# An encoder layer with mixture of experts: raw first rows with the norm in the copies, later small loads, an earlier overflow branch and a last norm in four pieces

## The chip, the cores and the metric

The kernel runs on one core of one Trainium2 chip. The metric is the device time of one execution in microseconds. It was 1304.65 us, the median of three runs (1300.25 to 1307.12).

## What is computed

One layer over 256 tokens of width 1024, in float32. A root-mean-square norm feeds a wide projection. Its parts go through a state-space branch (convolution over time, SiLU, two scan directions, gate) and an attention branch (8 query heads, 2 key/value heads, rotary angles). The two are gated and projected, and added to x. A second norm feeds a router that picks 4 of 32 experts for every token; each expert is two matrices with a clipped gated activation. The weighted sum is added to x, and a last norm gives the result.

```python
def rmsnorm(x, g):
    y = x * lax.rsqrt(jnp.mean(x * x, axis=-1, keepdims=True) + NORM_EPS)
    return y * g

def reference(x, ...):
    x = x + token_mixer(rmsnorm(x, g_mix), w_in, conv_w, ..., w_out)
    x = x + moe_ffn(rmsnorm(x, g_ffn), w_router, b_router, w_mlp1, b_mlp1, w_mlp2, b_mlp2)
    return rmsnorm(x, g_final)
```

## The kernel before

The five engines run programs of their own, written out by hand in one function, `encoder_layer`, and joined by semaphores. SP issues the large loads, ACT issues the small ones ahead of its own work, PE multiplies and transposes, ACT and DVE move results out of PSUM, and POOL computes the inverse roots (`rsqrt_mean`, L951 to L954: scale and add, then power).

Weights stream through `ring`, 16 slots of 1 MB. In the mixer ten slots are used, and the 36 units of the mixer (256 columns of a matrix with 1024 rows each) go through them in order (L333 to L337). SP starts with three waits: for x, for the five parameter rows and for b1. It issues ten units without a wait, then one for each unit that PE has finished. PE's `unit` (L420 to L437) multiplies a unit of weights with the transposed activations `hT` (L433) or the other way round (L436): 16 products of 256 columns, each of two instructions, into bank 0 or 1. A unit may start when ACT has taken the unit before the last one out of its bank (`unit_taken`).

The start is a chain. ACT issues x, the constants `cst` (736 KB), five parameter rows into `prm`, d_skip, b1, wdt, seven broadcast vectors and the router weights, L755 to L768. It squares both halves of x (L773), POOL makes the factors, DVE scales both halves into `hN` (L984), PE transposes 16 tiles of `hN` into banks 2 to 5 (`to_T`, L416), and DVE copies them out with g_mix into `hT` (`scaled_T`, L995), four copies of 128x512. Only then does unit 0 start. In front of `to_T` PE transposes the parameters (L400, L401) and b1 (L405, 16 transposes of 32 rows into bank 7). ACT copies those to `prmT` and `b1T` (L775, L777).

After the mixer comes the routing, and then the 32 experts, 12 units of 1 MB each, with SP keeping the ring full (L328). Eight of the units are the first matrix (`up_unit`) and four the second (`down_unit`); L629 holds their products, L663 the transposes of the result in between. The tokens of an expert are gathered by small products (L611), at most 64 of them per pass, and its output is added into banks 4 to 7 by `combine` (L624). More than 64 tokens for one expert would need a second pass; a flag `over_i` tells whether there is one, and each engine branches on it behind the experts (L924, L1304). With these inputs the pass isn't taken.

The end is a chain too. PE's last four `combine` products signal `c_psum`; DVE waits for all four, adds the banks to `xres` (L1288), reads the flag and branches (L1304), and signals ACT with a one-column copy (L1322). ACT squares both halves (L939), POOL makes the factors, DVE multiplies each half with factor and g_final (L1326), and SP stores each half when it is ready (L388, L390).

Of the kernel before, what the change touches and what calls it, by code (L numbers as in the profile page):

```python
# [7 lines left out]
ALU = mybir.AluOpType  # L8
# [3 lines left out]
P = 128  # L12
# [17 lines left out]
NE = 32  # L30
# [27 lines left out]
C_ID, C_LE, C_GE, C_ONE, C_NEGF, C_ZERO, C_NEGB = (P * i for i in range(7))  # L58
# [33 lines left out]
def encoder_layer(nc, x, g_mix, w_in, conv_w, conv_b, dt_bias_f, dt_bias_b, a_log_f, a_log_b, d_skip,  # L92
                  g_ssm, q_norm_g, k_norm_g, w_br_ssm, w_br_attn, w_out, g_ffn, w_router, b_router,
                  w_mlp1, b_mlp1, w_mlp2, b_mlp2, g_final, consts, out):
    with ExitStack() as ctx:
# [84 lines left out]
        gfin = arena[:, 5888:6912]  # L180
        msk = arena[:, 6912:6976].rearrange("p (t e) -> p t e", t=TT)
# [22 lines left out]
        c_in = sem("c_in"); x_in = sem("x_in"); row_in = sem("row_in"); b1_in = sem("b1_in")  # L204
# [5 lines left out]
        xsq_ready = sem("xsq_ready"); xr_ready = sem("xr_ready"); h_ready = sem("h_ready")  # L210
# [32 lines left out]
        over_step = sem("over_step"); over_left = sem("over_left"); over_even = sem("over_even")  # L243
        fsq_ready = sem("fsq_ready"); fr_ready = sem("fr_ready"); fin_ready = sem("fin_ready"); sum_done = sem("sum_done")
# [53 lines left out]

        def chain(eng, semaphore, base=0):
# [18 lines left out]
        def _(sp):  # L318
# [12 lines left out]
            sp.wait_ge(x_in, 16)  # L331
            sp.wait_ge(row_in, 16 * 5)
            sp.wait_ge(b1_in, 16)  # L333
# [53 lines left out]
            sp.wait_ge(fin_ready, 1)  # L387
            sp.dma_start(out[0, 0:P, :], hN[:, 0, :]).then_inc(out_done, 16)  # L388
            sp.wait_ge(fin_ready, 2)
            sp.dma_start(out[0, P:SEQ, :], hN[:, 1, :]).then_inc(out_done, 16)  # L390
            sp.wait_ge(out_done, 32)
# [3 lines left out]
        def _(pe):  # L395

            pe.wait_ge(c_in, 16)
            pe.wait_ge(row_in, 16 * 5)
            pe.wait_ge(dsk_ready, 1)
            nc.tensor.transpose(bank[6][:, 0:N_ROWS], prm[0:N_ROWS, :], ident[0:N_ROWS, 0:N_ROWS])  # L400
            nc.tensor.transpose(bank[6][:, N_ROWS:N_ROWS + 8], dske[:, :], ident[0:8, 0:8]).then_inc(prm_ready, 1)  # L401
            pe.wait_ge(b1_in, 16)
            for m in range(16):
                o = (m // KD) * KD + spot(m % KD)
                last = nc.tensor.transpose(bank[7][:, o * NE:(o + 1) * NE], b1raw[:, m * P:(m + 1) * P],  # L405
                                           ident[0:NE, 0:NE])
            last.then_inc(prm_ready, 1)

            def to_T(ready, psum_sem):

# [30 lines left out]
            for n in range(U_XBC, U_Z):  # L441
                unit(n, rhs=hT)
# [912 lines left out]
```

## Time and profile before

| | us |
|---|---|
| median of three runs | 1304.65 |
| lowest, highest | 1300.25, 1307.12 |
| span of the profiled execution | 1303.6 |
| PE busy | 1182.3 (91%) |
| PE weight loads busy | 578.6 (44%) |
| DVE busy | 364.2 (28%) |
| ACT busy | 193.1 (15%) |
| POOL busy | 19.9 (2%) |
| read from HBM | 443.61 MB, 341 GB/s over the span |
| share of the last chain | PE 40%, DMA 37%, SP's issues 16%, issue 2%, DVE 2% |

The profile is of one execution, and its times run from 0 at its first instruction to 1303.6 us. A busy share is a mean over stages with different limits. PE is busy for 91% of the span, yet in the last chain it has 40%, since in the long stage of the experts a product that waits for its weights and the stream of the weights take turns. L numbers are lines of the kernel. A wait in brackets behind a row is the idle time of the engine before it, and what ended it.

### The profile page before, as it was taken

How to read it: one execution, taken by the hardware profiler on the slowest of the kernel's cores; microseconds unless marked ns; L12 is line 12 of the kernel's file. 1: busy time of each engine (PE TensorE's matmuls, PEld its weight loads, DVE VectorE, ACT ScalarE, POOL GpSimd, SP SyncE). 2: the span in 40 equal slices, each digit the busy share in tenths (PEclk: the TensorE clock that was granted, in tenths of full speed). 3: DMA queues.
4: the chain of work that ended last, by engine and by line, in shares of the span. 5: the costliest groups of instructions: out<-in, count | busy, mean ns of one | idle time of the engine just before them, and what ended most of it. 6: DMA issues, size and time to landing. Idle time of an engine off the chain costs nothing.

```text
span 1303.6 us, 18034 instructions
## 1 busy us (share of the span) xinstructions
PE 1182.3 (91%) x6734; PEld 578.6 (44%) x6734; DVE 364.2 (28%) x1018; ACT 193.1 (15%) x362; POOL 19.9 (2%) x32
## 2 busy tenths in 40 slices
PE   5999999998799999989998988888899989998885
PEld 5888888887433333333333333333333333333331
DVE  2515788121412221222121111111122212111112
ACT  1212344001111110111011100100111011001001
POOL 0001111000000000000000000000000000000000
PEclk9999999999699999999999999999999999999998
DMA  9944322654099999999999999999999999999994
GB/s 283 281 142 117 128 97 97 230 217 171 29 417 417 417 417 417 417 417 418 417 418 418 418 418 418 418 418 417 417 417 418 418 418 418 418 418 417 418 417 178
DMA packets 113351, 445.18 MB, mean 342 GB/s; under 512 B 9731, under 2 KB 46947, under 8 KB 80515
## 3 DMA queue, kind: packets, MB, share of 16 engines
q1 hardware_dynamic: 109408, 441.48, 85.0%
q10 hardware_dynamic: 3907, 3.21, 0.9%
q8 instruction: 24, 0.39, 0.1%
q14 instruction: 12, 0.10, 0.0%
HBM read 443.61 MB, written 1.05 MB: 341 GB/s over the span
## 4 chain that ended last, share of the span: by engine, by line
PE 40%; DMA 37%; SPq 16%; issue 2%; DVE 2%; ACT 1%; ACTq 1%; DVEq 0%; POOL 0%; POOLq 0%
DMA ring<-in_w_mlp_dram 37%; SPq L328 16%; PE bank L433 14%; PE bank L629 14%; PE bank L436 5%; PE bank L624 1%; PE bank L611 1%; PE bank L562 1%; PE bank L552 1%; PE bank L698 1%; PE bank L524 1%; PE bank L416 1%; PE bank L663 0%; PE bank L591 0%; PE bank L515 0%
## 5 line engine op out<-in xcount | busy, mean ns | idle before, releaser
L629 PE MATMUL bank<-ring,arena 128*64 128x512 f32 x3072 | 702.7, 600 | 63.7 <-DMA ring<-in_w_mlp_dram 63.6
L629 PEld LDWEIGHTS bank<-ring,arena 128*64 128x64 f32 x3072 | 203.0, 137 | 515.3 <-issue 324.2
L1245 DVE TENSOR_TENSOR arena<-bank,b1T 128x256 f32<-128x256 f32 x128 | 53.8, 420 | 624.3 <-PE bank L663 621.9
L433 PE MATMUL bank<-hT,ring 128*128 128x256 f32 x576 | 128.3, 384 | 0.8 <-DVE hT L995 0.8
L433 PEld LDWEIGHTS bank<-hT,ring 128*128 128x128 f32 x576 | 110.9, 193 | 16.6 <-DVE hT L995 1.2
L436 PE MATMUL bank<-ring,hT 128*128 128x256 f32 x320 | 72.1, 386 | 2.2 <-DVE hT L1156 2.2
L906 ACT ACTIVATE arena<-bank 128x512 f32<-128x512 f32 x32 | 19.1, 597 | 362.4 <-PE bank L629 362.3
L436 PEld LDWEIGHTS bank<-ring,hT 128*128 128x128 f32 x320 | 61.5, 194 | 11.1 <-DVE hT L1156 2.6
L624 PE MATMUL bank<-arena 64*128 64x512 f32 x264 | 65.6, 615 | 0.8 <-ACT arena L916 0.8
L611 PEld LDWEIGHTS bank<-slotP,hb 128*128 128x128 bf16 x1536 | 47.7, 99 | 27.1 <-issue 23.5
L611 PE MATMUL bank<-slotP,hb 128*128 128x64 bf16 x1536 | 51.5, 195 | 3.1 <-DVE arena L1229 3.1
L663 PE MATMUL bank<-cst,arena 128*128 128x128 f32 x256 | 40.6, 286 | 14.4 <-ACT arena L906 9.6
L663 PEld LDWEIGHTS bank<-cst,arena 128*128 128x128 f32 x256 | 26.8, 140 | 47.1 <-ACT arena L906 36.1
L1227 DVE TENSOR_SCALAR slotP<-cst,rankm 128x64 bf16<-128x64 f32 x64 | 15.8, 247 | 96.9 <-ACT arena L914 96.9
L911 ACT ACTIVATE arena<-arena 128x256 f32<-128x256 f32 x64 | 26.7, 417 | 80.5 <-DVE arena L1248 80.4
L916 ACT ACTIVATE arena<-bank 128x512 f32<-128x512 f32 x32 | 19.1, 598 | 105.5 <-PE bank L629 105.5
L914 ACT ACTIVATE arena<-bank 128x256 f32<-128x256 f32 x32 | 12.3, 384 | 140.8 <-PE bank L618 140.8
L624 PEld LDWEIGHTS bank<-arena 64*128 64x128 f32 x264 | 22.7, 186 | 22.6 <-issue 20.9
L906 ACT ACT_TABLE_LOAD x8 | 10.3, 1283 | 134.4 <-PE bank L629 134.4
L433 PE MATMUL bank<-arena,ring 128*128 128x256 f32 x128 | 28.3, 380 | 0.5 <-ACT arena L867 0.5
L1251 DVE SCALAR_TENSOR_TENSOR arena<-arena 128x256 f32<-128x256 f32 x64 | 27.2, 426 | 2.4 <-DVE arena L1249 0.2
L433 PE MATMUL bank<-over,ring 128*128 128x256 f32 x128 | 27.8, 379 | 0.0
(204 smaller groups left out, 634.3 us busy)
## 6 DMA issues: line engine op xcount, KB each, us to landing
ring<-in_w_mlp_dram SPq DMA_DIRECT2D x384, 1024.0 KB, 22.1
ring<-in_w_in_dram SPq DMA_DIRECT2D x24, 1024.0 KB, 10.3
ring<-in_w_br_attn_dram SPq DMA_DIRECT2D x4, 1024.0 KB, 4.9
ring<-in_w_br_ssm_dram SPq DMA_DIRECT2D x4, 1024.0 KB, 5.0
ring<-in_w_out_dram SPq DMA_DIRECT2D x4, 1024.0 KB, 5.0
xres<-in_x_dram ACTq DMA_DIRECT2D x1, 1024.0 KB, 4.9
out_dram<-hN SPq DMA_DIRECT2D x2, 512.0 KB, 2.7
cst<-shape_constants_dram ACTq DMA_DIRECT2D x1, 736.0 KB, 6.4
```

The costliest lines, as they stand in the source:

```text
L328: sp.dma_start(dst, src).then_inc(slot_full[s], 16)
L433: last = nc.tensor.matmul(o, w[:, k, a * P:(a + 1) * P], rhs[:, k, :], start=(k == 0), stop=(k == KD - 1))
L436: last = nc.tensor.matmul(o, tokens[:, k, a * P:(a + 1) * P], w[:, k, :], start=(k == 0), stop=(k == KD - 1))
L611: last = nc.tensor.matmul(bank[b][:, k * CAP:(k + 1) * CAP], hb[part][:, t, k * P:(k + 1) * P], slotP[:, par, t, :], start=(t == 0 and par ...
L624: return nc.tensor.matmul(bank[b0 + q][:, :], slotWT[rows, (q // 2) * P:(q // 2 + 1) * P], ysb[rows, :], start=start, stop=stop, skip_grou ...
L629: return nc.tensor.matmul(bank[b][side * CAP:(side + 1) * CAP, :], tokens, w, start=start, stop=stop, skip_group_check=True)
L663: last = nc.tensor.transpose(bank[b][:, j * P:(j + 1) * P], hs[:, b * 512 + j * P:b * 512 + (j + 1) * P], ident)
L906: nc.scalar.activation(hs[:, 0:512], bank[0][:, :], ACT.Copy).then_inc(hs_ready, 1)
L911: nc.scalar.activation(sg[:, h * 256:(h + 1) * 256], ga[:, h * 256:(h + 1) * 256], ACT.Sigmoid, scale=ALPHA).then_inc(sg_ready, 1)
L916: nc.scalar.activation(ysb, bank[2][:, :], ACT.Copy).then_inc(ys_ready, 1)
L1245: step(V.tensor_tensor(o.rearrange("p (m s) -> p m s", m=4), bank[b][:, half].rearrange("p (m s) -> p m s", m=4), bias[:, m0:m0 + 4].unsqu ...
L1251: step(V.scalar_tensor_tensor(u_, u_, 1.0, g_, ALU.add, ALU.mult))
```

## The change

The start: SP drops its three waits and issues x itself, in two halves with a semaphore each, ahead of the weights. ACT first issues only the first 256 columns of the constants, now identity and ones, then the parameter rows and d_skip; b1, wdt, the vectors, the router weights and the rest of the constants are issued behind the squares and the parameter copy. A square of one column stands in front of the squares. PE transposes the raw x as its halves come. The factors of the norm reach the transposed side as a row: DVE writes them on two diagonals (`sqb`), PE multiplies ones with them, DVE copies the product into `rB`, and eight copies of 128x256 multiply the transposed x with g_mix and `rB`. Unit 0 (`first_unit`) goes through k outside and its two column halves inside, waiting for one copy at a time. The transposes of b1 move behind unit 3, and so does ACT's copy of them.

The end: the branch on the overflow flag stands in front of the sums on DVE, and the pass behind it uses banks 0 to 3 instead of 4 to 7. Sums, squares and stores go in four pieces of 128x512. The product with g_final is made on DVE before the factors are known, and the factors are then multiplied in by DVE for two pieces and ACT for two.

```diff
-C_ID, C_LE, C_GE, C_ONE, C_NEGF, C_ZERO, C_NEGB = (P * i for i in range(7))
+C_ID, C_ONE, C_LE, C_GE, C_NEGF, C_ZERO, C_NEGB = (P * i for i in range(7))
+C_FIRST = 2 * P
...
-            sp.wait_ge(x_in, 16)
-            sp.wait_ge(row_in, 16 * 5)
-            sp.wait_ge(b1_in, 16)
+            for t in range(TT):
+                sp.dma_start(xres[:, t, :], x[0, t * P:(t + 1) * P, :]).then_inc(x_in[t], 16)
...
+            for q in range(4):
+                sp.wait_ge(fin_ready[q], 1)
+                sp.dma_start(out[0, (q // 2) * P:(q // 2 + 1) * P, (q % 2) * 512:(q % 2 + 1) * 512], fin(hN, q)).then_inc(out_done, 16)
+            sp.wait_ge(out_done, 16 * 4)
...
+            pe.wait_ge(first_in, 16)
+            for t in range(TT):
+                pe.wait_ge(x_in[t], 16)
+                for k in range(KD):
+                    nc.tensor.transpose(bank[2 + k // 2][:, (k % 2) * 256 + t * P:(k % 2) * 256 + (t + 1) * P],
+                                        xres[:, t, k * P:(k + 1) * P], ident)
+            pe.wait_ge(row_in, 16 * 5)
+            pe.wait_ge(dsk_ready, 1)
+            nc.tensor.transpose(bank[6][:, 0:N_ROWS], prm[0:N_ROWS, :], ident[0:N_ROWS, 0:N_ROWS])
+            nc.tensor.transpose(bank[6][:, N_ROWS:N_ROWS + 8], dske[:, :], ident[0:8, 0:8]).then_inc(prm_ready, 1)
+            pe.wait_ge(xdiag_ready, 1)
+            nc.tensor.matmul(bank[7][:, 0:SEQ], ones, sqb, start=True, stop=True).then_inc(xrB_psum, 1)
+
+            def first_unit():
+
+                mix_full(pe, 0)
+                w = k_view(mix_slot(0))
+                for k in range(KD):
+                    pe.wait_ge(hT_ready, k + 1)
+                    for a in range(2):
+                        last = nc.tensor.matmul(bank[0][:, a * 256:(a + 1) * 256], w[:, k, a * P:(a + 1) * P], hT[:, k, :],
+                                                start=(k == 0 and a == 0), stop=(k == KD - 1), skip_group_check=True)
+                last.then_inc(unit_done, 1)
...
-            for n in range(U_XBC, U_Z):
+            first_unit()
+            for n in range(U_XBC + 1, U_Z):
                 unit(n, rhs=hT)
+                if n == U_XBC + 3:
+                    b1_transposes()
...
-            act.dma_start(xres[:, :, :], x[0].rearrange("(t p) d -> p t d", p=P)).then_inc(x_in, 16)
-            act.dma_start(cst[:, :], consts).then_inc(c_in, 16)
+            act.dma_start(cst[:, 0:C_FIRST], consts[:, 0:C_FIRST]).then_inc(first_in, 16)
...
+            act.wait_ge(pool_step, 2)
+            nc.scalar.activation(stat[:, 22:23], stat[:, 40:41], ACT.Square)
+            for t in range(TT):
+                act.wait_ge(x_in[t], 16)
+                nc.scalar.activation(hN[:, t, :], xres[:, t, :], ACT.Square, accum_out=stat[:, t:t + 1]).then_inc(xsq_ready, 1)
+            act.wait_ge(prm_ready, 1)
+            nc.scalar.activation(prmT[:, :], bank[6][:, 0:N_ROWS + 8], ACT.Copy).then_inc(prm_taken, 1)
             act.dma_start(b1raw, b_mlp1[0]).then_inc(b1_in, 16)
...
+            act.dma_start(cst[:, C_FIRST:N_CONST], consts[:, C_FIRST:N_CONST]).then_inc(c_in, 16)
...
+            for q in range(4):
+                act.wait_ge(c_added, q + 1)
+                nc.scalar.activation(fin(squares, q), fin(xres, q), ACT.Square, accum_out=stat[:, 28 + q:29 + q]).then_inc(fsq_ready, 1)
+            for t in range(TT):
+                act.wait_ge(fr_ready, t + 1)
+                act.wait_ge(xg_ready, 2 * t + 2)
+                nc.scalar.activation(fin(hN, 2 * t + 1), fin(hN, 2 * t + 1), ACT.Copy, scale=stat[:, 36 + t:37 + t]).then_inc(fin_ready[2 * t + 1], 1)
...
+            for t in range(TT):
+                pool.wait_ge(fsq_ready, 2 * t + 2)
+                link(nc.gpsimd.tensor_tensor(stat[:, 36 + t:37 + t], stat[:, 28 + 2 * t:29 + 2 * t], stat[:, 29 + 2 * t:30 + 2 * t], ALU.add))
+                rsqrt_mean(36 + t, 1, D).then_inc(fr_ready, 1)
...
             dve.wait_ge(xr_ready, 1)
-            for t in range(TT):
-                V.tensor_scalar(hN[:, t, :], xres[:, t, :], stat[:, t:t + 1], None, ALU.mult).then_inc(h_ready, 1)
-            dve.wait_ge(c_in, 16)
+            dve.wait_ge(first_in, 16)
+            for t in range(TT):
+                last = V.tensor_scalar(sqb[:, t * P:(t + 1) * P], ident, stat[:, t:t + 1], None, ALU.mult)
+            last.then_inc(xdiag_ready, 1)
+            dve.wait_ge(xrB_psum, 1)
+            link(V.tensor_copy(rB, bank[7][:, 0:SEQ]))
+            dve.wait_ge(prm_taken, 1)
+            for k in range(KD):
+                V.scalar_tensor_tensor(hT[:, k, :], bank[2 + k // 2][:, (k % 2) * 256:(k % 2 + 1) * 256], prmT[:, R_GMIX + k:R_GMIX + k + 1],
+                                       rB, ALU.mult, ALU.mult).then_inc(hT_ready, 1)
...
             dve.wait_ge(gfin_in, 16)
-            for t in range(TT):
-                V.scalar_tensor_tensor(hN[:, t, :], xres[:, t, :], stat[:, 30 + t:31 + t], gfin, ALU.mult, ALU.mult).then_inc(fin_ready, 1)
+            for q in range(4):
+                dve.wait_ge(c_psum, q + 1)
+                V.tensor_tensor(fin(xres, q), fin(xres, q), bank[SUMS + q][:, :], ALU.add).then_inc(c_added, 1)
+            dve.wait_ge(c_added, 4)
+            for t in range(TT):
+                for q in (2 * t + 1, 2 * t):
+                    V.tensor_tensor(fin(hN, q), fin(xres, q), gfin[:, (q % 2) * 512:(q % 2 + 1) * 512], ALU.mult).then_inc(xg_ready, 1)
+            dve.wait_ge(xg_ready, 4)
+            for t in range(TT):
+                dve.wait_ge(fr_ready, t + 1)
+                V.tensor_scalar(fin(hN, 2 * t), fin(hN, 2 * t), stat[:, 36 + t:37 + t], None, ALU.mult).then_inc(fin_ready[2 * t], 1)
```

## Rows read from the trace of the kernel before

**Rows 1.** The page's 40 equal slices: GB/s that the DMAs moved.
```profile
GB/s 283 281 142 117 128 97 97 230 217 171 29 417 417 417 417 417 417 417 418 417 418 418 418 418 418 418 418 417 417 417 418 418 418 418 418 418 417 418 417 178
```

**Rows 2.** Windows: length; busy PE, PEld, DVE, ACT, POOL; PEclk, DMA, GB/s.
```profile
352.00:355.00 3.00, 3.00 (x7) 0.77 (x8) 1.58 (x7) 0.00 (x0) 0.00 (x0) 0.50 0.00 0
358.00:362.00 4.00, 4.00 (x20) 1.26 (x18) 0.00 (x0) 0.00 (x0) 0.00 (x0) 1.00 1.01 397
```

**Rows 3.** Timeline, first 45 us: start, length, engine, line, operation, idle before.
```profile
0.73 0.44 ACTq L755 DMA_DIRECT2D xres<-in_x_dram  x1
...
3.76 0.32 ACTq L761 DMA_DIRECT2D dskr<-in_d_skip_dram  x1
...
8.95 1.28 ACT L773 ACT_TABLE_LOAD   x1 [8.95 <-issue]
9.29 0.21 DVE L979 COPY dske<-dskr 8x128 f32<-8x128 f32 x1 [9.29 <-DMA dskr<-in_d_skip_dram]
9.57 36.26 SPq L337 DMA_DIRECT2D ring<-in_w_in_dram  x13
...
10.10 1.89 PE L405 MATMUL bank<-cst,over 32*128 32x32 f32 x16
10.24 1.06 ACT L773 ACTIVATE hN<-xres 128x1024 f32<-128x1024 f32 x1
...
13.62 1.42 DVE L984 TENSOR_SCALAR hN<-xres,stat 128x1024 f32<-128x1024 f32 x2 [4.12 <-POOL stat L954]
...
15.10 3.67 PE L416 MATMUL bank<-cst,hN 128*128 128x128 f32 x16 [3.10 <-DVE hN L984]
...
19.55 25.79 PE L433 MATMUL bank<-hT,ring 128*128 128x256 f32 x108 [0.78 <-DVE hT L995]
```

**Rows 4.** DMA issues of the kernel: tile, engine, count, size, median us to landing.
```profile
ring<-in_w_out_dram SPq DMA_DIRECT2D x4, 1024.0 KB, 5.0
xres<-in_x_dram ACTq DMA_DIRECT2D x1, 1024.0 KB, 4.9
out_dram<-hN SPq DMA_DIRECT2D x2, 512.0 KB, 2.7
```

**Rows 5.** Landing of unit 0's weights, line L337, issued at 9.57.
```profile
DMA to landing us min/median/max: 9.0/9.0/9.0
```

**Rows 6.** Timeline of the tail, from 1288 us to the end.
```profile
1288.37 1.99 PE L624 MATMUL bank<-arena 64*128 64x512 f32 x8 [0.78 <-ACT arena L916]
...
1290.43 2.48 DVE L1288 TENSOR_TENSOR xres<-xres,bank 128x512 f32<-128x512 f32 x4 [8.35 <-PE bank L624]
1294.48 0.15 DVE L1322 COPY cnt<-cnt 128x1 f32<-128x1 f32 x1 [1.57 <-issue]
1294.66 1.06 ACT L939 ACTIVATE hN<-xres 128x1024 f32<-128x1024 f32 x1 [6.35 <-DVE cnt L1322]
...
1296.94 0.19 POOL L953 TENSOR_SCALAR stat<-stat 128x2 f32<-128x2 f32 x1 [973.61 <-ACT hN L939]
...
1297.94 2.48 DVE L1326 SCALAR_TENSOR_TENSOR hN<-xres,stat,arena 128x1024 f32<-128x1024 f32 x2 [3.31 <-POOL stat L954]
...
1300.45 0.36 SPq L390 DMA_DIRECT2D out_dram<-hN  x1
```

**Rows 7.** Groups by shape, DVE: line, operation, shapes, count, busy, mean ns.
```profile
L1127 DVE SCALAR_TENSOR_TENSOR over<-over,prmT,bank 128x256 f32<-128x256 f32 x8 | 3.8, 472 | 1.8 <-PE bank L552 1.8
...
L1145 DVE TENSOR_SCALAR arena<-cst,stat 128x128 f32<-128x128 f32 x2 | 0.5, 281 | 0.0
```

**Rows 8.** L433 alone in windows: length; busy PE, PEld; PEclk, DMA, GB/s.
```profile
19.55:24.05 4.50, 4.50 (x11) 3.60 (x12) 1.00 1.10 349
24.05:28.95 4.90, 4.90 (x24) 4.33 (x23) 1.00 1.10 348
```

**Rows 9.** Timeline, 214 to 217 us, one DVE line twice.
```profile
214.38 1.10 DVE L1099 TENSOR_TENSOR arena<-arena 128x512 f32<-128x512 f32 x1
...
216.69 0.69 DVE L1099 TENSOR_TENSOR arena<-arena 128x512 f32<-128x512 f32 x1
```

More of the change, by code:

```diff
@@ L180, in encoder_layer @@
         gfin = arena[:, 5888:6912]
+        squares = hs.rearrange("p (t d) -> p t d", t=TT)
         msk = arena[:, 6912:6976].rearrange("p (t e) -> p t e", t=TT)
@@ L203, in encoder_layer @@
         unit_done = sem("unit_done")
-        c_in = sem("c_in"); x_in = sem("x_in"); row_in = sem("row_in"); b1_in = sem("b1_in")
+        c_in = sem("c_in"); first_in = sem("first_in"); x_in = [sem(f"x_in{t}") for t in range(TT)]; row_in = sem("row_in"); b1_in = sem("b1_in")
         vec_in = sem("vec_in"); dsk_in = sem("dsk_in"); wdt_in = sem("wdt_in"); late_in = sem("late_in")
@@ L242, in encoder_layer @@
         over_y = sem("over_y"); over_ys = sem("over_ys"); over_c = sem("over_c"); over_added = sem("over_added")
-        over_step = sem("over_step"); over_left = sem("over_left"); over_even = sem("over_even")
-        fsq_ready = sem("fsq_ready"); fr_ready = sem("fr_ready"); fin_ready = sem("fin_ready"); sum_done = sem("sum_done")
+        over_wT = sem("over_wT"); over_step = sem("over_step"); over_left = sem("over_left"); over_even = sem("over_even")
+        fsq_ready = sem("fsq_ready"); fr_ready = sem("fr_ready"); fin_ready = [sem(f"fin_ready{q}") for q in range(4)]
         def mix_slot(n):
@@ L297, in k_view, with fin @@
             return ring[:, s, :].rearrange("p (k n) -> p k n", k=KD)
+        def fin(tile, q):
+            return tile[:, q // 2, (q % 2) * 512:(q % 2 + 1) * 512]
         def chain(eng, semaphore, base=0):
@@ L418, in to_T, with b1_transposes @@
                     last.then_inc(psum_sem, 1)
-            to_T(h_ready, hT_psum)
+            pe.wait_ge(first_in, 16)
[19 more added lines that the diff above has]
+                last.then_inc(unit_done, 1)
+            def b1_transposes():
+                pe.wait_ge(b1_in, 16)
+                for m in range(16):
+                    o = (m // KD) * KD + spot(m % KD)
+                    last = nc.tensor.transpose(bank[7][:, o * NE:(o + 1) * NE], b1raw[:, m * P:(m + 1) * P],
+                                               ident[0:NE, 0:NE])
+                last.then_inc(prm_ready, 1)
             def unit(n, rhs=None, tokens=None):
@@ L728, in _ @@
                                 o = spot(m % KD) * CAP
-                                last = nc.tensor.matmul(bank[4 + m // 8][:, o:o + CAP],
+                                last = nc.tensor.matmul(bank[m // 8][:, o:o + CAP],
                                                         ring[:, k, m * P:(m + 1) * P], x32[:, k, :],
@@ L738, in _ @@
                                 o = (k % 2) * D + side * 512
-                                last = half_product(0, side, act32[:, spot(k), :], ring[:, k // 2, o:o + 512],
+                                last = half_product(2, side, act32[:, spot(k), :], ring[:, k // 2, o:o + 512],
                                                     k == 0, k == KD - 1)
@@ L793, in _ @@
                     silu(u - 1)
+                if u == 3:
+                    b1_copy()
             silu(5)
@@ L929, in _ @@
                         act.wait_ge(over_x, n)
-                        nc.scalar.activation(slotWT, bank[7][:, 0:256], ACT.Copy)
+                        nc.scalar.activation(slotWT, bank[2][:, 0:256], ACT.Copy).then_inc(over_wT, 1)
                         act.wait_ge(over_ga, n)
```

60 lines of the change are left out of this document (16 added, 44 removed).

## The prediction

> **What bounds the kernel now.** I read four views in this order. The slices of the page come first [rows 1]. From the twelfth slice to the last but one the DMA engines move 417 to 418 GB/s without a gap: this is the stream of 32 experts' weights, 12 MB each. It starts when the PE gives back the first ring slot of expert 0. In the window from 352 to 355 us nothing moves, and from 358 us it is 397 GB/s [rows 2]. From there to the last weights the stream never pauses, so the end of the kernel is the time of that first release, plus a constant, plus what follows the last weights. Two stretches are therefore worth money one for one: the chain up to the experts, and the tail.
>
> The chain up to the experts is a dependency chain, not a transfer. Its start is in the timeline of the first 20 us [rows 3]. ACT spends the time up to 8.95 us issuing small loads, loads its table (1.28 us) and starts the first square at 10.24 us, though x had landed 4.9 us after its issue at 0.73, at about 5.6 us [rows 4]. Then come POOL, two DVE scalings at 13.62, sixteen PE transposes at 15.10, four DVE copies, and the first projection unit starts at 19.55 us. It waited for hT, not for weights: SP issued the first weights at 9.57 us and they landed 9.0 us later, at 18.57 [rows 3, 5]. From then on PE is the busiest engine of the mixer, and DVE and ACT work in its wake, so a start that is S us earlier moves the whole mixer by S.
>
> The tail is in the timeline after 1288 us [rows 6]: PE combines from 1288.37 to 1290.36, four DVE sums from 1290.43 (waiting for all four products), the overflow branch on DVE (1.57 us idle before the copy at 1294.48), two ACT squares, POOL, two DVE scalings from 1297.94, and stores, the last issued at 1300.45 and landing 2.7 us later [rows 4].
>
> **The head, step by step.** SP now issues x's two halves at about 0.7 and 1.2 us and the first weights at about 1.7. ACT issues only the first 256 columns of the constants, five parameter rows and d_skip. That is the list up to the d_skip issue, which ran from 3.76 to 4.08, less one issue of x at 0.44 [rows 3]: ACT is free at about 3.6. Then:
> - table load 1.28 and a one-column square of some 0.2: 5.1 us. The whole x landed at 5.6 alone in its queue; its first half should be there by about 4.4 and the second by 6;
> - two squares and POOL, 3.4 us, as now from 10.24 to DVE's start at 13.62: 8.5 (the squares end at about 7.3);
> - two diagonals 128x128, 0.28 each or 0.5 together [rows 7]: 9.0;
> - PE's product of ones with 256 columns. Two such instructions at the low clock take 11 in 4.50 us, so 0.43 each [rows 8], plus the drain: 1.2: 10.2;
> - DVE copies the broadcast row out of PSUM. The nearest row is the 128x256 copy-multiply at 0.47 [rows 7]: 10.7;
> - the first of eight scaled copies, 0.47: 11.2. Unit 0 needs only that one to start. Its four instructions per k take PE 1.7 us at the low clock and 0.86 at the full one, more than 0.47, so DVE stays ahead.
>
> PE's other work lies under this: sixteen transposes of raw x, 3.67 us [rows 3], from about 4.5 as the halves land to about 8.2, and the two parameter transposes behind them. D_skip was used at 9.29 before because it queued behind x and all constants; now it has 128 KB ahead of it in its own queue, and has until about 8 us. Unit 0 starts at 11.2 instead of 19.55: **8.3 us earlier**.
>
> The weights of unit 0 must be there by then. A 1 MB load of that shape lands 5.0 us after issue when the queue is empty [rows 4] and 9.0 in the crowd at 9.57 [rows 5]. Issued at 1.7 behind 1 MB of x, which takes 2.6 us at 410 GB/s, that is 9.3, at worst 13.3. I take 9.3, since the eleven small loads that made the crowd are now issued only after the parameter copy. The price at the worst end is 2.1 us.
>
> The b1 transposes move from a gap before hT to behind unit 3, where PE has no gap. They took 1.89 us at the low clock [rows 3]; at the full one between half of that, 0.95, and all of it. I take **1.1 us lost**. ACT's b1 copy behind them is covered by its long waits for units. The eleven late issues, constants' rest included, take 5.2 us, as eleven did from 3.76 to 8.95 [rows 3]: from 8.6 to about 14; the next ACT work is unit 0's copy, at 28.97 less 8.3. If they were slow to issue, the cover is 6 us. DVE's bf16 identity and selector now come behind hT, in a gap of 10 us.
>
> The clock: unit 0 ran 11 instructions in its first 4.50 us and 24 in the next 4.90 [rows 8]. That is 1.2 GHz and then 2.4, although the clock column reads 1.00 throughout there. The low part cost about 2.2 us against a full-clock start. I take the same loss again; the bounds are 2.2 gained (full clock at once) and 4.5 lost (unit 0 wholly low, 32 instructions at 0.43 instead of 0.216, less the 2.2). A second such place is the entrance of the experts: 7 instructions in 3.0 us at a granted 0.50 in the window 352 to 355 against 20 in 4.0 us at 1.00 [rows 2]. If the rise comes 3 us later or earlier, half of it is lost or won: 1.5 us. Head: 8.3 - 1.1 = **7.2 us**.
>
> **The tail.** The branch instructions leave the path: DVE has been idle since the last activations and takes the branch there, ACT takes it after its last copy. That removes 1.57 us. The sums start at the first product instead of the last. The four products take 1.99 us, so the first is out at about 1289.0, and the sums run from 1289.1, at 0.6 each as now [rows 6], to 1291.6 instead of 1292.9. The squares follow piece by piece, 0.65 to 0.75 each (two whole ones took 2.28 to POOL's start at 1296.94): the last ends at 1292.5. POOL adds one operation per half and then has 1.0 us as now: the two factors at about 1292.5 and 1293.7. DVE's four products with g_final, not made before, take 4 x 0.6 in the meantime, to 1294.1. The last scalings end at about 1295.0 on DVE and 1294.9 on ACT. Four store issues of 0.36 from 1294.6 put the last one at 1295.8, against 1300.45. Its landing takes 2.7 as before, less up to 0.6 for half the bytes. I take the full 2.7 because four stores queue. **4.7 us**; from 3.7 (POOL and DVE in each other's way, below) to 5.4.
>
> In 214 to 217 us a DVE product of two SBUF operands took 1.10 us while POOL worked beside it and 0.69 without it [rows 9]. The tail now puts four such products beside POOL's small ones, which costs 0 to 0.8. A rule speaks against this part of the change: the Trainium skill, GPSIMD Engine Reference, Specifications, says that GpSimd shares its SBUF interfaces with VectorE and contends with instructions that have two SBUF inputs. By the rule with the row's price on two products, the tail gives 3.9 instead of 4.7.
>
> **Sum.** 7.2 + 4.7 = 11.9 us off the profiled span of 1303.6: 1291.7. The median of the three times is 1304.65, 1.05 above this span; the same 11.9 off it is **1292.7**. The three times spread from 1300.25 to 1307.12.
>
> **Rivals.**
> - The head is held by loads. For: a load of 1 MB took 9.0 us in the crowd and 5.0 alone [rows 4, 5]; now every parameter row and d_skip has the weight queue beside it. If d_skip or unit 0's weights come 4 to 6 us late, unit 0 starts at 15 to 17 and the sum is 11.9 - 5: 1297.7. Against: there are only some hundred small packets. A rule fits this: the Trainium skill, DMA: Bandwidth & Descriptors, Queues, rings and completion order, says that each engine takes turns between queues by whole packets of several descriptors, so that a small load waits for more than one of the other's. By it d_skip would be later than its queue position says. Chance 0.13.
> - The tail gives little. ACT or DVE reaches its branch late, or the stores follow each other at their full 2.7. Then only some 2 us of the 4.7 are left: 1295.4. Chance 0.08.
> - The change doesn't do what it says at the head: the start of unit 0 moves, but the mixer loses it again, because another chain (conv on DVE, late small loads) sets the experts' start. Only the tail is left: 1300. Against: the first units leave ACT and DVE gaps of 2 to 6 us. Chance 0.08.
> - Slower: the clock at the entrance of the experts. At 0.43 us an instruction, as from 352 to 355 [rows 2], a weight unit of eight takes 3.4 us, and the stream brings 1 MB in 2.5, so each unit at the low clock starves the stream by 0.9. The clock rises about 3 us after the start of expert 0 now. If the changed timing kept it low for 13 units, the gain of 11.9 would be gone; for 20 units the kernel is 6 us slower; I price it at 1311. Nothing in the trace shows the clock low under such work for long. Chance 0.05.
>
> **How the numbers follow.** Forecast 0.66, with a range of its own from 1288.5 to 1297 (both clock places together 3.5 either way, weights 2.1, tail 1, the spread of the runs). Range for all: 1287 to 1300, which takes in the first three rivals and leaves out the slower one and what lies beyond the best bounds. A measurement of this kernel tells about 0.5%, 6.5 us, from no change. Faster by more than that, below 1298.1, is the forecast, the tail rival and somewhat over half of the load rival: 0.81. Within it: 0.13. Slower: 0.06.
>
> **What would show it.** In the new trace: the first square at about 5.1 us, unit 0 at about 11.2 with its release by hT; the transposes of b1 behind unit 3 at about half their old length; the first DMA traffic of the experts' stream 7 us earlier; the last weights 7 us earlier; no idle stretch of 1.57 on DVE behind the sums; the last store issued about 7.5 us after the first combine instead of 12.1. Wrong would be a wait of PE for ring or for dske before unit 0, a later rise of the clock, or a mixer whose length from unit 0 to the experts has grown by more than 1 us.

## The result and the profile after

The changed kernel took 1296.66 us in the median of five runs (1288.9 to 1297.44), the kernel before on the same chip 1306.26 (1300.25 to 1307.12). The ratio is 0.9923 with a 95% interval of 0.9896 to 0.9951: about 10 us faster. The forecast was 1292.7 with a range of 1287 to 1300. The profiled execution has a span of 1292.7 us, 10.9 less than the 1303.6 of before; the sum had said 11.9. Of the runs of the kernel before that stand beside the experiments one took 2429.91 us; it counts as a slow run and is left out of the ratios.

Two lines of the page of the changed kernel: the granted clock in tenths (9 is 90% or more) and the GB/s of the DMA engines, in 40 equal slices of 32.3 us.

```profile
PEclk9999999999699999999999999999999999999999
...
GB/s 304 295 131 131 131 98 103 254 202 130 77 418 417 416 417 417 417 417 418 418 418 418 418 418 418 418 418 418 417 417 417 417 418 418 418 418 417 417 417 231
```

The experts' stream is as full as in [rows 1], and it begins earlier in the eleventh slice, which holds 77 GB/s instead of 29. It hands on most of what was gained before it: the seventeenth load of the experts, the first that waits for PE, is issued 7.5 us earlier (348.41 instead of 355.87), the first combine comes 7.0 us earlier. Of the start, the timeline of the changed kernel (start, length, engine, line, operation, idle before) shows:

```profile
0.73 0.87 SPq L338 DMA_DIRECT2D xres<-in_x_dram  x2
...
1.65 44.92 SPq L342 DMA_DIRECT2D ring<-in_w_in_dram  x14
...
3.66 1.28 ACT L788 ACT_TABLE_LOAD   x1 [3.66 <-issue]
...
5.05 3.67 PE L416 MATMUL bank<-cst,xres 128*128 128x128 f32 x16 [5.05 <-DMA cst<-shape_constants_dram]
5.06 1.04 ACT L791 ACTIVATE hN<-xres 128x1024 f32<-128x1024 f32 x1
...
8.26 0.21 DVE L1015 COPY dske<-dskr 8x128 f32<-8x128 f32 x1 [8.26 <-DMA dskr<-in_d_skip_dram]
8.55 0.48 DVE L1021 TENSOR_SCALAR arena<-cst,stat 128x128 f32<-128x128 f32 x2
...
10.64 3.23 DVE L1027 SCALAR_TENSOR_TENSOR hT<-bank,prmT,arena 128x256 f32<-128x256 f32 x8
...
11.27 7.14 PE L432 MATMUL bank<-hT,ring 128*128 128x256 f32 x32 [1.13 <-DVE hT L1027]
...
19.44 0.60 ACT L818 ACTIVATE arena<-bank 128x512 f32<-128x512 f32 x1 [9.93 <-issue]
...
39.07 1.18 PE L441 MATMUL bank<-cst,over 32*128 32x32 f32 x16
```

Unit 0 starts at 11.27 us instead of 19.55 [rows 3], released by hT, 0.63 us after the first of eight copies began. Its 32 instructions take 7.14 us: it ran at the full clock, 2.4 GHz, from its first one, where its first 11 instructions had run at 1.2 GHz before [rows 8]. The b1 transposes stand behind unit 3 and take 1.18 us.

The tail, from the first combine on, in the same columns:

```profile
1281.39 1.99 PE L650 MATMUL bank<-arena 64*128 64x512 f32 x8 [0.78 <-ACT arena L946]
1282.62 2.48 DVE L1364 TENSOR_TENSOR xres<-xres,bank 128x512 f32<-128x512 f32 x4 [7.52 <-PE bank L650]
...
1285.13 2.50 DVE L1368 TENSOR_TENSOR hN<-xres,arena 128x512 f32<-128x512 f32 x4
...
1285.31 0.92 POOL L988 TENSOR_TENSOR stat<-stat 128x1 f32<-128x1 f32 x1
...
1287.16 1.02 POOL L988 TENSOR_TENSOR stat<-stat 128x1 f32<-128x1 f32 x1
1287.66 1.05 DVE L1372 TENSOR_SCALAR hN<-hN,stat 128x512 f32<-128x512 f32 x2
1288.18 1.83 SPq L394 DMA_DIRECT2D out_dram<-hN  x4
```

It answers to [rows 6]: the first store is issued 6.79 us after the first combine instead of 10.9, the last at 8.17 instead of 12.1, and lands 10.9 us after it instead of 14.8.

So the profiled difference of 10.9 us is 7.0 at the first combine (1288.37 to 1281.39) and 3.9 behind it.

### The profile page after: what moved, and what is told of

Read it like the earlier page. It is cut to its first block, busy times and chain, and to the rows that moved or that the text cites. A ratio compares the mean times of both kernels' runs of the same rounds, so it can differ in the third digit from the quotient of the medians.

```text
span 1292.7 us, 18065 instructions
## 1 busy us (share of the span) xinstructions
PE 1182.5 (91%) x6736; PEld 578.1 (45%) x6736; DVE 365.1 (28%) x1026; ACT 195.3 (15%) x369; POOL 22.4 (2%) x36
## 4 chain that ended last, share of the span: by engine, by line
PE 51%; DMA 26%; SPq 18%; issue 3%; DVE 2%; ACT 1%; POOL 0%; POOLq 0%; ACTq 0%; DVEq 0%
DMA ring<-in_w_mlp_dram 25%; PE bank L655 21%; SPq L334 17%; PE bank L456 14%; PE bank L459 5%; PE bank L650 2%; PE bank L637 2%; PE bank L689 1%; PE bank L588 1%; PE bank L578 1%; PE bank L432 1%; PE bank L724 1%; PE bank L550 1%; PE bank L644 0%; PE bank L617 0%
## 5 line engine op out<-in xcount | busy, mean ns | idle before, releaser
L456 PE MATMUL bank<-hT,ring 128*128 128x256 f32 x544 | 121.0, 383 | 0.0
L456 PEld LDWEIGHTS bank<-hT,ring 128*128 128x128 f32 x544 | 104.4, 192 | 14.4
L944 ACT ACTIVATE arena<-bank 128x256 f32<-128x256 f32 x32 | 12.3, 384 | 140.9 <-PE bank L644 140.9
## 6 DMA issues: line engine op xcount, KB each, us to landing
cst<-shape_constants_dram ACTq DMA_DIRECT2D x1, 608.0 KB, 15.3
```

The costliest lines, as they stand in the source:

```text
L456: last = nc.tensor.matmul(o, w[:, k, a * P:(a + 1) * P], rhs[:, k, :], start=(k == 0), stop=(k == KD - 1))
```

## The experiments

Theory A, which the expectations name, is this: the change saves a fixed time at each end, and what differs from run to run is how many stretches of PE fall to the low clock in the mixer. The rivals were that the start's gain is lost in the mixer, that the ends themselves vary, and that the loads hold the start. Of the twelve kernels tried, five undo or isolate a part, one repeats the changed kernel, and six take a further step. Below, "tail" with a number is the time from the first combine of the end to the landing of the last store. Five kernels ran only once: the branch put back took 1296.80 us, the fused scaling 1293.56, the weights held back 1297.56, the small loads early 1301.42, beside 1304.28 for one run of before, and the last one below 1294.55. These times alone show no difference of a few us; what is read of these runs is the rows of their traces.

**The changed kernel again.**

> The changed kernel once more, beside the kernel before. Theory A (the gain is a fixed amount of time at both ends, and what moves from run to run is how many short stretches at the low TensorE clock fall into the mixer): about 10 us faster than before in the median; its profile has unit 0's first product at 11.3 us and 10.9 us from the first combine to the last store's landing, the same as the first profile within 0.3, while the number of low-clock stretches between unit 0 and the experts differs. The lower mean clocks go with the longer spans, 1.7 us for each 3.4 us at half clock. Rival (the two ends themselves vary, with DMA latency): unit 0 or the tail differ by over 1 us between the two profiles.

1294.66 us in the median of six runs against 1304.77 for before: ratio 0.993 (0.9909 to 0.995). Unit 0 started at 11.48, and the last store landed 10.9 us after the first combine, so the two profiles agree at both ends to 0.2 us. The end stays so fixed: 10.9 in every profile with this tail. The start does not: in the six profiles of kernels that issue their first loads in this same way unit 0 begins between 11.27 and 12.15 us. The low stretches did not differ here (the profile's clock record has the same five, each 0.4 us later), so this pair shows nothing of their part; the further profiles below do.

**The start alone, the end alone.**

> Only the change at the start, with the old tail. Theory A: unit 0 at 11.3 us, the tail from first combine to the last store's landing 14.8 us as before, and 7 us faster than before (ratio 0.9945), 3 us more or less by low-clock stretches. Rival (the gain at the start is lost in the mixer and the measured gain comes from the tail): within 2 us of before.

> Only the change at the end, with the old start. Theory A: unit 0 at 19.5 us, 10.9 us from the first combine to the last landing instead of 14.8, and 4 us faster than before (ratio 0.997). Rival: 8 us or more faster, if the start gives nothing.

Each is the kernel before with the lines of one end of the diff. The start alone: 1296.96, ratio 0.9935 (0.9912 to 0.9958), 7.8 us; unit 0 at 11.36, tail 14.8. The end alone: 1300.72, ratio 0.9973 (0.996 to 0.9986), 4.1 us; unit 0 at 19.57, tail 10.9. The two sum to 11.9 where the whole change gave 10.1 on the same chip; the intervals are wide enough for that. The start's gain is not lost on the way, so that rival falls.

**The branch put back.** Edit: the reading of the flag and the branch stand behind DVE's four sums again (the pass inside the branch is cut here).

```diff
-            OSTEPS = TT + 3
-            dve.wait_ge(route_ready, 1)
-            again = dve.value_load(over_i[0:1, 0:1], min_val=0, max_val=1)
...
             for q in range(4):
                 dve.wait_ge(c_psum, q + 1)
                 V.tensor_tensor(fin(xres, q), fin(xres, q), bank[SUMS + q][:, :], ALU.add).then_inc(c_added, 1)
             dve.wait_ge(c_added, 4)
+            OSTEPS = TT + 3
+            dve.wait_ge(route_ready, 1)
+            again = dve.value_load(over_i[0:1, 0:1], min_val=0, max_val=1)
...
```

> The changed kernel with DVE's reading of the overflow flag and its branch put back behind the four sums. Theory A: 1.6 us more between the sums and DVE's first product with g_final, and the whole of it, 1.4 to 1.6 us, at the last store, since DVE's chain of sums, products and scalings sets the first store. Rival (POOL's second factor sets the end): DVE has slack, and the last landing moves by under 0.7 us.

Its tail in the timeline:

```profile
1282.19 1.99 PE L650 MATMUL bank<-arena 64*128 64x512 f32 x8 [0.78 <-ACT arena L946]
...
1286.12 0.55 POOL L988 TENSOR_TENSOR stat<-stat 128x1 f32<-128x1 f32 x1
...
1287.34 0.56 POOL L988 TENSOR_TENSOR stat<-stat 128x1 f32<-128x1 f32 x1
1287.45 2.50 DVE L1368 TENSOR_TENSOR hN<-xres,arena 128x512 f32<-128x512 f32 x4 [1.55 <-issue]
...
1290.50 1.83 SPq L394 DMA_DIRECT2D out_dram<-hN  x4
```

The first store is issued 8.31 us after the first combine instead of 6.79, and the last lands at 12.4 instead of 10.9: the branch is worth its whole 1.5 us, and DVE's chain sets the first store. The rows also show something that was not asked. POOL's first power operation has DVE idle beside it and takes 0.55 us, where it took 0.92 and 1.02 in the changed kernel beside DVE's products of two SBUF operands. The second one begins 0.11 us before such a product, runs beside it for most of its time, and still takes 0.56. So a product beside it is not enough: in the slow cases the product had begun before the power operation.

**Fewer products in the tail.** Edit: the early products are made for ACT's two pieces alone, and ACT waits for one product per half; DVE multiplies its own pieces with both factors at once.

```diff
-                act.wait_ge(xg_ready, 2 * t + 2)
+                act.wait_ge(xg_ready, t + 1)
...
             for t in range(TT):
-                for q in (2 * t + 1, 2 * t):
-                    V.tensor_tensor(fin(hN, q), fin(xres, q), gfin[:, (q % 2) * 512:(q % 2 + 1) * 512], ALU.mult).then_inc(xg_ready, 1)
-            dve.wait_ge(xg_ready, 4)
+                V.tensor_tensor(fin(hN, 2 * t + 1), fin(xres, 2 * t + 1), gfin[:, 512:1024], ALU.mult).then_inc(xg_ready, 1)
             for t in range(TT):
                 dve.wait_ge(fr_ready, t + 1)
-                V.tensor_scalar(fin(hN, 2 * t), fin(hN, 2 * t), stat[:, 36 + t:37 + t], None, ALU.mult).then_inc(fin_ready[2 * t], 1)
+                V.scalar_tensor_tensor(fin(hN, 2 * t), fin(xres, 2 * t), stat[:, 36 + t:37 + t], gfin[:, 0:512], ALU.mult, ALU.mult).then_inc(fin_ready[2 * t], 1)
```

> The changed kernel with half of the early products with g_final: DVE makes them only for ACT's two pieces, and for its own two multiplies with factor and g_final in one instruction once the factor is there. Theory A (the tail was 0.8 us longer than predicted because DVE's four early products come before its first scaling and slow POOL down beside them): POOL's two power operations fall from 0.92 and 1.03 us towards 0.55 to 0.7, the first store is issued about 1.2 us earlier after the first combine (5.6 instead of 6.8), and the last lands about 1 us earlier: 9.8 to 10.1 us after the first combine instead of 10.9. Rival (four store issues one after another on SP set the end anyway, or POOL is as slow without them): under 0.4 us.

```profile
1281.44 1.99 PE L650 MATMUL bank<-arena 64*128 64x512 f32 x8 [0.78 <-ACT arena L946]
...
1285.36 0.92 POOL L988 TENSOR_TENSOR stat<-stat 128x1 f32<-128x1 f32 x1
...
1287.16 2.31 SPq L394 DMA_DIRECT2D out_dram<-hN  x4
1287.27 0.56 POOL L988 TENSOR_TENSOR stat<-stat 128x1 f32<-128x1 f32 x1
...
1287.86 0.75 DVE L1370 SCALAR_TENSOR_TENSOR hN<-xres,stat,arena 128x512 f32<-128x512 f32 x1 [0.73 <-POOL stat L988]
```

The first store comes 5.72 us after the first combine and the last lands at 9.9: 1.0 us gained, as expected. The power operations were expected to fall both, and one did: the first still follows the start of a product and still takes 0.92; the second has none and takes 0.56. POOL's first factor is no earlier (4.8 us after the first combine in both), so the first store's gain comes from DVE's shorter chain and not from a faster POOL. Now DVE waits 0.73 us for POOL's second factor: POOL has become the bound of the second half of the tail, which it was not before.

**Weights held back until the parameter rows have landed.** Edit: one line, `sp.wait_ge(row_in, 16 * 5)`, between x and the weights.

> The changed kernel with one of SP's old waits put back: weights only after the five parameter rows have landed (about 7 us). Theory A: the rows land a little earlier, unit 0's weights are issued at about 6.5 to 7 us and land 5 to 9 us later, so unit 0 starts at 12 to 15 us instead of 11.3, waiting for ring. Rival (weights were never near the path): unit 0 at 11.3 us.

```profile
7.06 0.21 DVE L1016 COPY dske<-dskr 8x128 f32<-8x128 f32 x1 [7.06 <-DMA dskr<-in_d_skip_dram]
...
12.46 9.46 PE L433 MATMUL bank<-hT,ring 128*128 128x256 f32 x32 [2.32 <-DMA ring<-in_w_in_dram]
```

Unit 0 waits for its weights and starts at 12.46. In the changed kernel they landed at 9.3, 2.0 us before their use. Here they were issued 5.2 us later and landed 5.6 us after that instead of 7.6, at 12.4: this used up the 2.0 and cost 1.2 more. The same run shows the other side. Without the weight queue beside it, d_skip is used at 7.06; with it, at 8.26, 8.11, 7.86, 8.91, 9.33 and 8.29 in the other profiles with this order.

**The small loads early again.** Edit: b1, wdt, the vectors, the router weights and the rest of the constants are issued before the first square.

> The changed kernel with b1, wdt, the vectors, the router weights and the rest of the constants issued before the squares again. Theory A (ACT's issuing time sets the start): the first square comes 5.5 us or more later, at 10.5 to 14 us, and unit 0 starts that much later, 17 us or later. Rival (d_skip's landing at 8.3 us or the diagonals set it): unit 0 moves by less than 3 us.

```profile
10.00 0.21 DVE L1015 COPY dske<-dskr 8x128 f32<-8x128 f32 x1 [10.00 <-DMA dskr<-in_d_skip_dram]
...
16.47 1.04 ACT L799 ACTIVATE hN<-xres 128x1024 f32<-128x1024 f32 x1
...
22.73 3.75 PE L432 MATMUL bank<-hT,ring 128*128 128x256 f32 x8 [1.13 <-DVE hT L1027]
```

The first square comes at 16.47, later than the 14 expected at most, and unit 0 at 22.73. These eleven issues take 10.8 us here, from 4.21 to 15.03: 7.0 for the first ten, which took 4.8 in the kernel before with no weights under way, and 3.8 for the rest of the constants alone (608 KB). Moving the small loads behind the squares is the part without which the weights' early start would have made things worse: unit 0 would be 3.2 us later than before the change.

**The dt products among others.** In the changed kernel the low-clock stretch of 3.4 us from 57.6 follows the small products of the dt columns (54.10 to 57.6). They are 16 products of 32 columns, in 32 instructions; the "32 products" of the expectation are these instructions. In this run each product stands behind one of the first z unit.

> The changed kernel with its 32 small products for dt (32 columns each, 3.65 us together, in front of the z units) put between the products of the first z unit. In the first profile of the changed kernel the low-clock stretch from 57.6 to 61.0 us follows exactly these products and costs 1.7 us. Theory A (PE's rare use of the array during them lowers the clock, whenever they fill the time before a decision): no low-clock stretch there in any profile, a mean clock a little higher, and 1 to 2 us faster than the changed kernel in the median. Rival (the stretch has nothing to do with them): the stretch comes as often and the time is the same.

Windows of the changed kernel (length; busy of PE, weight loads, DVE, ACT, POOL; clock, DMA, GB/s), and of this run:

```profile
54.10:57.50 3.40, 3.40 (x33) 3.40 (x31) 2.49 (x6) 1.11 (x2) 0.00 (x0) 1.00 1.09 344
57.60:61.00 3.40, 3.40 (x10) 2.77 (x10) 2.05 (x6) 0.63 (x1) 0.00 (x0) 0.50 0.66 217
```
```profile
54.00:58.00 4.00, 4.00 (x21) 3.56 (x20) 1.51 (x4) 0.58 (x2) 0.00 (x0) 1.00 0.73 240
58.00:62.00 4.00, 4.00 (x25) 3.68 (x25) 3.81 (x10) 0.53 (x2) 0.00 (x0) 1.00 0.88 259
```

PE was busy by the column in both, yet the clock was halved behind the first and not in the second. 1292.41 us in the median (1290.23 to 1294.16), ratio 0.9905 (0.9886 to 0.9925), 2.2 us under the changed kernel beside it. Unit 0 began 0.7 us later than in that kernel's profile, so its start is not what made it faster. A second pair follows.

**Further steps together.**

> The changed kernel with four further steps: the dt products between those of the first z unit, DVE's own pieces scaled by one instruction with both factors, ACT issuing the stores of its own two pieces, and d_skip issued before the parameter rows. Theory A: d_skip is used by DVE at 7.5 us or earlier (8.3 to 9.3 in the profiles so far), unit 0 starts at 11.0 to 11.4; no low-clock stretch between 50 and 70 us; the last landing is 9.2 to 9.6 us after the first combine instead of 10.9; in the median 1290.5, 3 to 4 us under the changed kernel and 14 under before. Rival (what d_skip gains the parameter rows lose, as they now come last): PE's parameter transposes wait until 8.5 us or later and unit 0 doesn't move.

> The same with the dt products together again, in front of the z units: a second look at what they do to the clock. Theory A: 1 to 2 us slower in the median than the version with them in between, and where its profile has a low-clock stretch between 50 and 70 us, it follows these products. Rival (the 2.2 us of the first comparison were chance): the two medians agree within 1 us.

With the dt products in between 1291.66 us, ratio 0.9903 (0.9889 to 0.9917); without 1293.9, ratio 0.991 (0.9891 to 0.9928): again 2.2 us. Each pair's intervals overlap, so the size is not settled. The stretch itself: in eleven profiles with the products together it was there five times, and in the three with them in between never. If the edit did nothing, three profiles without the stretch would still come with a chance of about one in six (6/11 three times over). That the dt products bring the stretch about is not shown, only likely.

Three expectations missed. The median is 12.3 us under before, not 14. The last landing came 10.2 us after the first combine and not 9.2 to 9.6: with ACT issuing two stores it is later than the 9.9 with all four on SP. And d_skip, now issued first, is used at 5.06, but the parameter rows take its place at the edge. The version with the old dt products started unit 0 at 12.50, since

```profile
9.60 0.42 PE L420 MATMUL bank<-cst,prm 96*128 96x96 f32 x1 [0.91 <-DMA prm<-in_conv_w_dram]
```

while its sister had them at 8.46 and started at 11.43. The rival of the first of these runs (what d_skip gains, the rows lose) holds in one of two profiles.

**Only unit 0's weights ahead of the rows.**

```diff
             for n in range(N_MIX):
+                if n == 1:
+                    sp.wait_ge(row_in, 16 * 5)
```

> The dt products in between, fused scaling with all four stores on SP, d_skip ahead of the parameter rows, and SP issuing only unit 0's weights before the parameter rows have landed, the other units behind them. In the profiles so far d_skip or the rows landed between 7.1 us (weights held back) and 9.6 us (weights beside them), and unit 0 started at 11.3 to 12.5 us. Theory A (small loads beside the weight queue decide the last microsecond of the start): the rows are used by 8.5 us, unit 0 starts at 11.2 to 11.5 with no wait for prm or dskr before it, the last landing is 9.9 us after the first combine, and the median is 1290 to 1291.5. Rival (1 MB of weights in front is enough to hold the rows back as before, or unit 1 now comes too late): a wait for prm before unit 0, or a wait for ring before unit 1.

> The changed kernel with only the two steps at the start (d_skip first, the second and later weights behind the rows). Theory A: unit 0 at 11.2 to 11.5 us again, PE's parameter transposes right behind those of x (8.5 us), no wait for ring before unit 1; tail 10.9. Rival: as for the other run of this call.

Unit 0 started at 11.47 and 11.31, with the rows used at 8.57 and 8.41 and no wait for ring behind it. The rival is half right: SP's issue behind its wait shows that the rows landed by 8.54 and 8.21, 5.3 and 5.0 us after the issue of the last row. With no weights in front it was 4.1 us (2.79 to 6.85). So 1 MB of weights does hold them back, by about 1 us. It does not move unit 0, since PE's product of ones follows at 9.12 and 8.96, as in the changed kernel (9.15). The first kernel has 1290.81 us in the median (1288.73 to 1293.55), ratio 0.9892 (0.9872 to 0.9913), the lowest median here: about 13 us under before. Against the 1291.66 of the version with split stores that is no difference. The second, run once, has a tail of 10.9 and a span of 1292.7.

**What the clock did in all of them.** For ten of the fourteen profiles: the start of unit 0, the time from there to the issue of the experts' seventeenth load (the first that waits for PE), the low-clock time in the mixer up to 300 us by the profile's clock record, and the distance less half of that time. Before the first entry of the record the low clock is read from the spacing of unit 0's instructions. Half of the low-clock time is what it costs, if PE is busy all through it.

| kernel | unit 0 | to 17th load | low clock | distance less half |
|---|---|---|---|---|
| before | 19.55 | 336.3 | 7.9 | 332.4 |
| the end alone | 19.57 | 334.1 | 3.4 | 332.4 |
| changed | 11.27 | 337.1 | 6.8 | 333.7 |
| changed, again | 11.48 | 337.3 | 6.8 | 333.8 |
| the start alone | 11.36 | 337.9 | 9.8 | 332.9 |
| fused scaling | 11.53 | 337.7 | 9.6 | 332.9 |
| late weights | 12.46 | 339.7 | 11.5 | 333.9 |
| dt between | 12.15 | 336.2 | 4.6 | 333.9 |
| further, old dt | 12.50 | 339.5 | 11.2 | 333.9 |
| both further | 11.43 | 333.8 | 0.0 | 333.8 |

The distance moves by 6 us between profiles; less half the low-clock time it is 332.4 with the old start, and 332.9 or 333.8 with the new one, 0.5 to 1.5 more, in which b1's 1.1 must lie. Which of the two it is goes with where the long low stretch at the routing begins: at 318 us in the two profiles with 332.9, at 321 to 328 in the others with the new start. Of the four profiles left out, three fit the first group (332.7 to 332.9, with that stretch at 318). The small loads early does not: 330.6, with a long stretch of 13.7 us where all others have 23.9. The mixer does not lose the start's gain to another chain; what varies there between profiles is mostly the clock.

That the clock also makes the spread among runs of one kernel is shown in part only. The changed kernel's fastest run, 1288.9, has the highest mean clock, 0.987, and the other four have 0.981 to 0.984. But of the twelve runs of the end alone eleven have the same mean clock, 0.986, and they spread from 1298.9 to 1302.7. Some 4 us of spread have another cause, which stays open.

## Why the prediction was right, and where it was off

| step | predicted | profile of the changed kernel |
|---|---|---|
| first square | 5.1 | 5.06 |
| DVE's diagonals | 8.5 | 8.55 |
| unit 0's weights landed | 9.3 | 1.65 + 7.6 = 9.3 |
| first copy to hT | 10.7 | 10.64 |
| unit 0 starts | 11.2 | 11.27 |
| b1 on PE's path | 1.1 | 1.1 |
| ACT's late issues done | 14 | 19.3 |
| gain at the first combine | 7.2 | 7.0 |
| first sum after the first combine | 0.7 | 1.2 |
| first and second factor | 4.1, 5.3 | 4.8, 6.8 |
| first and last store issued | 6.2, 7.4 | 6.8, 8.2 |
| gain of the tail | 4.7 | 3.9 |

The chain at the start held to 0.1 us at the steps in the table, since each had a row of the same instruction or of one near it, and the runs of the start alone and the end alone bear out the two parts of the sum: 7.8 and 4.1 us. The clock term was off inside its bounds: I took the same loss again, but unit 0 ran at full clock (2.2 us gained) and a low stretch came behind the dt products (1.7 lost). By these terms the seventeenth load should come 7.7 us earlier, 8.3 - 1.1 + 2.2 - 1.7, and it came 7.5 earlier. Another 0.5 was lost between it and the first combine, a distance that the sum took as constant: it was 932.5 us before and 933.0 now, and lies between 932.2 and 933.3 in the fourteen profiles. So the net 7.0 agrees with 7.2 in part by luck. In nine of the other profiles unit 0 ran at the low clock for its first 3 to 6 us.

The tail was 0.8 us short. Three terms were mis-sized. The first product was taken as a quarter of the 1.99 us, but the first sum starts 1.23 us after the first combine and the products come out in two pairs: 0.5 us. The stores were issued 0.46 us apart, not 0.36: 0.3 us over three of them. And POOL's factors came 0.7 and 1.5 us late, 0.5 of it by the late first sum. The contention had been priced at up to 0.8 on DVE; it fell on POOL, whose power operation went from 0.55 to 0.92 and 1.02, while DVE's four products took 0.68 to 0.69 each. The rule named there, from the Trainium skill (GPSIMD Engine Reference, Specifications), agrees with the trace in that the two engines hinder each other; which one pays was read wrongly from one row.

The trace of before had the answer. It holds the DVE line of [rows 9] 16 times and the POOL line beside it 8 times (shortest, median and longest in ns):

```profile
L1099 DVE TENSOR_TENSOR arena<-arena x16: 691/691/1099, 151.7 to 227.1; 128x512 f32<-128x512 f32 x16
...
L963 POOL TENSOR_TENSOR arena<-arena x8: 722/1226/1234, 160.8 to 231.5; 128x256 f32<-128x256 f32 x8
```

The 1.10 us of [rows 9] is the only one of the sixteen that is not 0.69 or 0.70. There POOL's instruction had begun first, by 0.30 us (it took 0.86), and DVE's product was slowed. In six other places DVE's product had begun first, and POOL's instruction took 1.23 us instead of the 0.72 that it took with DVE idle. In the tail, too, DVE's products begin first. The later of the two was the slower one each time, except for the second power operation with the branch put back, where neither was.

This cost almost nothing in the changed kernel, because DVE's own chain ended late enough to cover it. Its products ended at 1287.63 and its first scaling at 1288.15; the second factor came at 1288.19. Once DVE's chain had been made shorter, DVE waited 0.73 us for the factor. So the tail of 3.9 us that the prediction gives by the rule is the measured 3.9 by luck: the missing 0.8 is the first sum and the store issues, not the contention.

The measured median lies 4 us above the forecast, at 1296.66. 1.6 of that is the kernel before, whose median was 1306.26 with five runs, not 1304.65. 0.8 is the tail's terms and 0.2 the start's. The rest, 1.4, lies within the spread of the runs. On repetition the gain was 10.1.

Of the rivals, the one with loads at the start is partly true. The loads of d_skip and of the rows sit on the edge: used up to 9.3 and 9.6 us, they cost 0.6 to 1.2 us in three of the profiles (unit 0 at 11.87, 12.15 and 12.50) and nothing in the others. D_skip was used at 7.06 without weights beside it and at 7.9 to 9.3 with them. The rule cited for it, from the Trainium skill (DMA: Bandwidth & Descriptors, Queues, rings and completion order), agrees with this in kind; no run shows how the DMA engines take turns. The weights themselves landed early, 2.0 us before their use. The mixer rival fell with the start alone, 7.8 us. The tail rival (a loss of 2.7) and the slower one (a low clock at the experts' entrance) did not occur; the low stretch there lasts 23.9 us in the profile of before and in that of the changed kernel.

One cover was thinner than stated. ACT's late issues took 10.1 us instead of 5.2 beside the weight queue, and its copy of unit 0 came at 19.44, behind the unit's end at 18.4. PE didn't notice, because it needs that copy only for the unit after next.

## What to carry to other kernels

Where a stream bound by DMA follows a dependency chain, every microsecond of the chain counts in full, so the first 20 us and the last 15 are the places to look; price each link by a row of the same instruction. When large loads are moved ahead, count the small loads that are waited for early: they land later and their issues take longer beside a full queue, and only those needed first may stay in front. In a tail that is cut in pieces, watch what a product of two SBUF operands does to POOL beside it, and try folding a scaling into one instruction rather than making the product early; here that gave 1.0 us. Before a contention is priced from one row, look at every instance of that line: here six of the seven with both engines at work said the opposite.

## What the runs showed of the hardware

- PE can be busy for all of a stretch by the busy column and still be granted 1.2 GHz behind it: the 32 instructions of 32 columns each, busy for all of 54.10 to 57.50 us, were followed by 3.4 us at 0.50. This happened in five of eleven profiles.
- The power operation on POOL, 128x1, took 0.55 us with DVE idle and 0.92 to 1.02 beside DVE products of two SBUF operands that had begun before it; a scale-and-add went from 0.19 to 0.51. A power operation that began 0.11 us before the product took 0.56.
- A POOL instruction on 128x256 took 0.72 us with DVE idle and 1.23 when a DVE product of two SBUF operands (0.69 us) had begun before it. Where POOL's had begun first, DVE's product took 1.10.
- The last four products, of 64 rows each, finish in two pairs: the first sum on DVE began 1.23 us after the first of them, where all four take 1.99.
- Ten small DMA issues on ACT took 4.8 us with an empty weight queue and 7.0 beside a full one. The load of 608 KB behind them took 3.8 us to issue and, in the changed kernel, 15.3 to land.
- A first load of 1 MB behind 1 MB of x landed 7.6 us after its issue.
